# One order of work for the gate products, the decay steps and the fourth modulation sum of a hybrid RG-LRU / SGU / conv-FFN block

## What is computed

```python
mod = silu(c) @ w_ada + b_ada                      # six vectors of 1024
h = modulated_norm(x, norm_mix_g, shift1, scale1)
xr, gr, zu, zv, ga, gb = split(h @ w_in)
xr = causal_dwconv(xr, rnn_conv_w, rnn_conv_b)     # four taps
r = sigmoid(block_diag(xr, lru_w_a, lru_b_a))      # 8 heads, 128 x 128 each
i = sigmoid(block_diag(xr, lru_w_x, lru_b_x))
log_a = 8 * r * log_sigmoid(lam)
a = exp(log_a)
u = sqrt(-expm1(2 * log_a)) * (i * xr)
h_t = a_t * h_(t-1) + u_t                          # scan over the tokens
y_a = (h * gelu(gr)) @ w_branch_a
y_b = spatial_gating(gelu(zu), gelu(zv)) @ w_branch_b
x = x + gate1 * ((sigmoid(ga) * y_a + sigmoid(gb) * y_b) @ w_out)
# then the channel sub-layer: norm, up, conv(3), gelu * val, down, gate2, final norm
```

## Time and profile before

| | |
|---|---|
| time, median of 3 runs | 1642.93 us (1642.1 to 1643.86) |
| the profiled execution's own time | 1643.54 us |
| its span in the trace | 1641.8 us |
| busy, TensorE / its weight loads | 1572.3 us (96%) / 1296.6 us (79%) |
| busy, VectorE / ScalarE / GpSimd | 1104.0 us (67%) / 712.2 us (43%) / 347.8 us (21%) |
| mean granted TensorE clock | 0.976 |
| moved by DMA | 146.10 MB |

### The profile page before, as it was taken

How to read it: one execution, slowest core, us unless ns; L and a number is a source line. 1 busy time by engine, 2 the same in 40 slices (tenths; PEclk the granted TensorE clock), 3 DMA queues, 4 the chain that set the end, 5 groups by cost and what they waited for, 6 DMA issues and landing times.

```text
span 1641.8 us, 18632 instructions
## 1 busy us (share of the span) xinstructions
PE 1572.3 (96%) x6996; PEld 1296.6 (79%) x6996; DVE 1104.0 (67%) x1209; ACT 712.2 (43%) x974; POOL 347.8 (21%) x218
## 2 busy tenths in 40 slices
PE   5889999999999999998999899999999999999998
PEld 4667777778888888887887778888888888888886
DVE  6877888855565684465437986677667667567674
ACT  3446878744555461111123434334334334334436
POOL 0432433532222200000000411211221221121204
PEclk7789999999999999998999999999999999999999
DMA  9322222221233347666210012112111111211112
GB/s 355 120 77 64 75 74 74 71 87 54 91 103 103 103 135 228 205 189 209 93 52 26 20 52 77 40 54 63 51 46 58 58 46 52 65 39 52 52 45 103
DMA packets 154312, 146.10 MB, mean 89 GB/s; under 512 B 6672, under 2 KB 132976, under 8 KB 153584
## 3 DMA queue, kind: packets, MB, share of 16 engines
q1 hardware_dynamic: 154224, 144.91, 27.8%
HBM read 123.91 MB, written 20.97 MB: 88 GB/s over the span
## 4 chain that ended last, share of the span: by engine, by line
PE 75%; DVE 13%; issue 4%; ACT 3%; DMA 3%; POOL 1%; SPq 0%; POOLq 0%; ACTq 0%; DVEq 0%
PE ps L671 42%; PE ps L929 15%; PE ps L728 11%; DVE wop L1495 2%; DMA ada_ring<-in_w_ada 2%; DVE xc L1649 1%; PE ps L959 1%; PE ps L859 1%; PE ps L800 1%; DVE ti L1681 1%; PE ps L647 1%; DVE t3w L2015 1%; DVE m L1672 1%; PE ps L633 1%; PE ps L749 1%
## 5 line engine op out<-in xcount | busy, mean ns | idle before, releaser
L1495 DVE TENSOR_TENSOR wop<-raw,wop 128x512 fp32r<-128x512 f32 x423 | 320.1, 766 | 220.3 <-ACT wop L1007 217.7
L1007 ACT ACTIVATE wop<-raw 128x512 fp32r<-128x512 f32 x423 | 260.8, 626 | 476.4 <-PE ps L671 151.2
L671 PE MATMUL ps<-yq,wop 128*128 128x512 f32 x1716 | 419.9, 394 | 14.0 <-DVE wop L1495 7.2
L671 PEld LDWEIGHTS ps<-yq,wop 128*128 128x128 f32 x1716 | 326.3, 191 | 85.6 <-DVE hidw L1967 4.9
L929 PE MATMUL ps<-hid,wop 128*128 128x512 f32 x1056 | 241.1, 389 | 0.0
L929 PEld LDWEIGHTS ps<-hid,wop 128*128 128x128 f32 x1056 | 198.2, 188 | 41.2
L530 POOL TENSOR_TENSOR raw<-raw,raw 128x512 f32<-128x512 f32 x45 | 66.7, 1482 | 493.1 <-DVE wop L1495 444.2
L1989 DVE SCALAR_TENSOR_TENSOR xT<-ps,mod,xT 128x1024 f32<-128x1024 f32 x88 | 113.0, 1284 | 47.0 <-PE ps L929 46.0
L671 PE MATMUL ps<-t2q,wop 128*128 128x512 f32 x540 | 132.7, 395 | 6.3 <-DVE wop L1495 6.1
L671 PE MATMUL ps<-t4q,wop 128*128 128x512 f32 x540 | 131.0, 391 | 2.2 <-DVE ps L1508 2.0
L1967 DVE SCALAR_TENSOR_TENSOR hidw<-ps,pc,hidw 128x1023 f32<-128x1023 f32 x96 | 122.8, 1279 | 13.2 <-ACT hidw L1367 12.3
(11 more groups left out here) (214 smaller groups left out, 1826.5 us busy)
## 6 DMA issues: line engine op xcount, KB each, us to landing
raw<-in_w_in SPq DMA_DIRECT2D x96, 256.0 KB, 3.3
raw<-in_w_up SPq DMA_DIRECT2D x96, 256.0 KB, 2.8
ada_ring<-in_w_ada SPq DMA_DIRECT2D x32, 512.0 KB, 4.4
raw<-in_w_down SPq DMA_DIRECT2D x48, 256.0 KB, 2.9
gate_keep<-tg SPq DMA_DIRECT2D x16, 512.0 KB, 4.1
tg<-gate_keep SPq DMA_DIRECT2D x16, 512.0 KB, 6.7
xtok<-in_x SPq DMA_DIRECT2D x4, 1024.0 KB, 6.8
ada_h<-in_w_ada SPq DMA_DIRECT2D x8, 512.0 KB, 9.0
```

What stands on the lines that cost most here:

```text
L671: done = nc.tensor.matmul(bank, left[:, w, lk, :], right[:, x, rk, :], start=(first and w == 0 and x == 0), stop=(last and w == 1), skip_g ...
L1007: nc.scalar.activation(wop[n % 4][:, 0, :, :], raw[slot][:, :, :], ACT.Copy).then_inc(f_hi, 1)
L1495: V.tensor_tensor(wop[n % 4][:, 1, :, :], raw[slot_of[n][0]][:, :, :], wop[n % 4][:, 0, :, :].bitcast(F32), ALU.subtract).then_inc(f_lo, 1)
```

## The change

In the units that follow an R unit, the gate products go between P3 and P4 in place of P2 and P3, and with them `gate_pair` and `decay` from slot 3 to slot 4. `decay_root` goes from slot 1 to slot 2. On VectorE, `decay_square` goes from slot 6 to slot 1 of the next unit, behind the conv taps and their split, `gated_input` from slot 3 to slot 5, `scan_input` from slot 2 to slot 3, and the splits that stood together in slot 6 go back to their slots, between the joins. On ScalarE, `hi` of the next unit's product 1 goes inside `decay`. In the projections, the fourth weight load of a unit goes ahead of the gate's and of the modulation's loads on the queue, and the fourth vector (e=3) is spread over B1 and B2, its sum being moved from B2 to B3. No instruction is added or removed, and none changes its size. The diff, cut to its core:

```diff
@@ tables
+        SUMS_AT = {AT["A", 2]: 0, AT["A", 3]: 1, AT["B", 1]: 2, AT["B", 3]: 3}
@@ sync engine, loop over the units
                 if g is not None:
                     spill_gate(g, 1)
+                weights(pos, 3, 4)
                 if SEQ[now][0] in "AB":
                     gate_back(SEQ[now][1] + (4 if SEQ[now][0] == "B" else 0))
                 if now in ADA_AT:
-                    ada_pieces(ADA_AT[now], 2, 8)
-                weights(pos, 3, 4)
+                    ada_pieces(ADA_AT[now], 2, 6 if ADA_AT[now] == 3 else 8)
+                if SEQ[now] == ("B", 2):
+                    ada_pieces(3, 6, 8)
                 if pos in ADA_AT:
                     ada_pieces(ADA_AT[pos], 0, 2)
@@ tensor engine
-                m, b, e = prev_unit(now, "R"), V_BLOCK[now] if now in V_BLOCK else None, ADA_AT[now - 1] if now - 1 in ADA_AT else None
+                m, b, e = prev_unit(now, "R"), V_BLOCK[now] if now in V_BLOCK else None, SUMS_AT[now] if now in SUMS_AT else None
...
-                if m is not None and w == 3:
+                if m is not None and w == 4:
                     block_diag(m, past)
...
-                    if s == 1 and pos - 1 in ADA_AT:
-                        e = ADA_AT[pos - 1]
+                    if s == 1 and pos in SUMS_AT:
+                        e = SUMS_AT[pos]
@@ scalar engine
-            def decay(m):
+            def decay(m, weights, n):
...
                 nc.scalar.activation(th[:, :], la_a[:, :], ACT.Tanh, bias=la4n[:, m:m + 1],
                                      scale=la4n[:, m:m + 1]).then_inc(ach, 1)
+                weights(n)
                 act.wait_ge(ach, 2 * m + 1)
...
-                    hi(n0 + w + 3)
+                    if m is None or w < 5:
+                        hi(n0 + w + 3)
                     if m is not None and w == 1:
                         conv_high(m)
-                    if m_past is not None and w == 1:
+                    if m_past is not None and w == 2:
                         decay_root(m_past)
-                    if m is not None and w == 3:
+                    if m is not None and w == 4:
                         gate_pair(m, BANKS[(pos - 1) % 2])
-                        decay(m)
+                        decay(m, hi, n0 + 8)
+                    if m is not None and w == 6:
+                        hi(n0 + 9)
@@ vector engine, units
                 for w in range(7):
+                    if m is not None and w == 5:
+                        gated_input(m)
                     if w >= 4:
                         join(pos, w - 4)
...
+                    if m_past is not None and w == 1:
+                        decay_square(m_past)
                     if m_past is not None and w == 3:
+                        scan_input(m_past)
                         scan(m_past)
...
-                    if m is None or w < 4:
-                        lo(n0 + w + 3)
-                    elif w == 6:
-                        lo(n0 + 7)
-                        lo(n0 + 8)
-                        decay_square(m)
-                        lo(n0 + 9)
+                    lo(n0 + w + 3)
...
-                    if m_past is not None and w == 2:
-                        scan_input(m_past)
-                    if m is not None and w == 3:
-                        gated_input(m)
@@ vector engine, branch projections
-                    if w == 2 and pos - 1 in ADA_AT:
-                        mod_part(ADA_AT[pos - 1], BANKS[(pos - 1) % 2][0])
+                    if w == 2 and pos in SUMS_AT:
+                        mod_part(SUMS_AT[pos], BANKS[(pos - 1) % 2][0])
                     if pos in ADA_AT:
                         e = ADA_AT[pos]
-                        for k in range(4 * (w - 2), 4 * (w - 2) + 4) if e % 2 and w >= 2 else range(2 * w, 2 * w + 2) if e % 2 == 0 else ():
+                        late = 2 if e == 3 else 4
+                        for k in range(late * (w - 2), late * (w - 1)) if e % 2 and w >= 2 else range(2 * w, 2 * w + 2) if e % 2 == 0 else ():
                             ada_piece(e, k)
+                    if SEQ[pos] == ("B", 2) and w < 2:
+                        ada_piece(3, 4 + 2 * w)
+                        ada_piece(3, 5 + 2 * w)
```

## The result

| | before | after |
|---|---|---|
| time, median of 4 runs | 1643.09 us (1642.10 to 1643.86) | 1619.96 us (1619.49 to 1621.60) |
| the profiled execution's own time | 1643.54 us | 1621.60 us |
| its span in the trace | 1641.8 us | 1619.9 us |
| mean granted TensorE clock | 0.976 | 0.978 |

The account below looks back on a forecast made before the run. The prediction took a ring over VectorE, ScalarE and GpSimd as the R stage's bound. The ring's 10.8 us plus the fourth sum's 9.6 made 20.4 us off, from the median of 1642.9 to 1622.5 us; range 1616.5 to 1631.

Parts of the forecast that it names:

- The reading of the bound: R stage: the 24.07 us unit period is set by VectorE, ScalarE and GpSimd; TensorE's holes are only its shadow.
- the ring: R stage: almost gapless chain of steps over VectorE, ScalarE and GpSimd, from one unit's conv taps to the next's, 24.07 us.
- The ring's length: R stage after the change: 12.2 plus 10.24 us, taken as 22.5 a unit; eight units give 10.8 us less.
- the hole at P6: R unit on TensorE: P6 would wait for join 1, which ends about +19.6 where P6 could start at +19.04: 0.6 us.
- The fourth sum: Projections: moving the fourth column sum to B3 removes 5.8 us of wait and 3.8 of slow clock, 9.6 us less.
- The queue at nothing: A and B units: sending the fourth weight load ahead of gate loads and pieces was put at no gain or loss.
- the units behind at nothing, with 1 us either way: One or two units behind the R stage, finishing the last head: decay_square in their first slots costs nothing, give or take 1 us.
- TensorE is the bound again: Rival, R stage: VectorE and GpSimd meet less, ring under 21.76 us, 25.6 us less in all, 1617.3 us; chance 0.17.
- three meetings in a unit of the old order: R stage: VectorE and GpSimd already contend three times in every old unit, the argument against TensorE being the bound.
- The ring stays longer: Rival, R stage: decay_square still contested, 1.1 us more, ring 23.6 us, 12.7 us less in all, 1630.2 us; chance 0.15.
- Only one half works: Rival: either the ring gains nothing (1633.3 us) or the fourth sum waits or slows another transfer (about 1632); chance 0.08.
- Slower: Rival, R stage: GpSimd gets ahead at three more meetings, 1.14 us each, ring 25.9 us, 1646.3 us; chance 0.03.

Follow-up runs that it names:

- decay_only: Kernel before with only decay_square moved behind the conv's split and decay_root one slot later; gate products stay between P2 and P3: 1632.86 us, ratio 0.9938.
- products_back: Changed kernel with only the gate products put back between P2 and P3 on TensorE: 1624.09 us, ratio 0.9887 to before.
- products_only: Kernel before with only the gate products moved behind P3 on TensorE, ScalarE and VectorE as before: 1655.7 us, ratio 1.008.
- short_y: Changed kernel with GpSimd's product of scan and gelu gate cut to 16 of its 1024 columns, the others left without the gate: 1616.15 us, ratio 0.9838.
- queue_only: Kernel before with only the fourth weight load moved ahead of the gate's and modulation's loads on the queue: 1643.53 us, ratio 1.0005.
- sum_old_queue: Kernel before with the fourth vector spread over B1 and B2 and its sum in B3, fourth weight load left behind the pieces: 1633.39 us, ratio 0.9948.
- y_on_vector: Changed kernel with the product of scan and gelu gate moved from GpSimd to VectorE, between join 2 and the last split: 1615.62 us, ratio 0.984.
- the two halves: Two runs: kernel before with only the modulation and queue part, 1633.88 us; changed kernel with that part undone, 1630.18 us.

## Why the prediction was right

**The reading of the bound.** Right. `decay_only` leaves the gate products where they wait and gives 10.0 us, and `products_back` puts them back into the changed kernel and loses some 2. `products_only` removes the wait and costs 12.8, though partly by a new wait of its own. The waits of the earlier trace rows were the shadow of the ring.

**The ring's length.** Worked out as 22.4 and taken as 22.5; measured 22.49 (199.84 to 222.33). The first part, from the taps to the start of GpSimd's product behind the scan, was 12.2 in the sum and is 12.16 (212.00 - 199.84), the second 10.24 and is 10.33. The steps came as worked out: `decay_square` 1.23 forecast and 1.22 measured, the split behind join 0 about 2.3 and 2.31, the hole at P6 0.6 and 0.51. The eight units gave 10.97 us for a forecast of 10.8; the first interval is 21.76 and the other six 22.47 to 22.59.

The Trainium skill (SBUF — State Buffer, on who interferes with whom) has a VectorE instruction with two SBUF inputs and a GpSimd one that reads SBUF take a shared port pair as a lock that the first holds to its end. The trace after agrees at the five meetings from `L565` on (ends at 215.32, 216.47, 217.55, 218.69, 219.24). `short_y` falls to TensorE's 21.76 us, which fits too but doesn't prove the lock, as the weight sums behind the short product also start earlier.

**The fourth sum.** Forecast 9.6 us, 5.8 of wait and 3.8 of low clock; measured 9.70 between the two landmarks, 5.84 of idle time and 3.86 (61.95 - 58.09) of the same matmuls taking longer. The pieces are in place 13.7 us ahead where I had reckoned with over 15.

**The queue at nothing.** Right, by `queue_only` and `sum_old_queue`.

**What was off.** The term "the units behind at nothing, with 1 us either way" was mis-sized: ZV1 gave 1.49 us. I had asked only whether the added `decay_square` found room, and not what the moves free. The unit is 0.43 us ahead at P2 (6.24 in place of 6.67 us from its start), 0.98 at P3 (9.06 in place of 10.04) and 1.50 at P6, whose wait of 0.24 us for a join went too. Only the step from P2 to P3, some 0.5 us, is the root's later slot: a copy that P3 waits for no longer stands behind it. `decay_only`, which moves the root and `decay_square` alone, gives 0.60 in ZV1 and nothing at P2. The 0.43 at P2 is there in `products_back` too (6.24), so it comes with what that run has and `decay_only` hasn't, the new order of splits, joins, gates and `gated_input`. ScalarE starts its reading of the V tiles (L1186, now L1190) 2.76 us into the unit in place of 3.68, and P2's copy stands behind it:

```profile
325.54 1.94 ACT L1186 ACTIVATE vv<-ps 128x1024 f32<-128x1024 f32 x2
```

```profile
313.55 1.94 ACT L1190 ACTIVATE vv<-ps 128x1024 f32<-128x1024 f32 x2
```

The dependence of P3 on its copy was also missing from my expectation for `products_only`, which came out 7 us worse. With that term, 0.2 us on the ring, 0.1 on the sum, and 0.4 us that the part from O0 on gave back (its cause is open), 20.4 becomes 21.8 of the 21.9 us between the two profiled executions. The medians differ by 23.1; the profiled execution of after is the slowest of its four runs, and the 1.2 us between the two measures lie within the runs' own spread.

**The rivals.** "TensorE is the bound again" needed the meetings to cost 0.74 us less a unit. They didn't; one product moved from GpSimd to VectorE is enough for it, as `y_on_vector` shows. I had counted three meetings in a unit of the old order against this rival; the earlier trace rows show five (`gated_input`, L530, `decay_square`, L541 and the last split each end behind the other engine's), so that argument was stronger than I made it. "The ring stays longer" fell with `decay_square` at 1.22 us. "Only one half works" fell with the two halves. "Slower" happened, but in `products_only` and by another mechanism than the one named: not meetings on SBUF, but a copy behind the root.

## What to carry to other kernels

Several small waits of the busiest engine, one in each unit and all alike, may be the shadow of a ring over engines none of which is busy all the time (here VectorE for 84%, ScalarE for 80% and GpSimd for 42% of a unit). Follow the work from one unit's instruction to the same one in the next: if there is no gap, the period is the ring's, and only what shortens the ring helps. Moving the waiting instruction alone can lengthen it, as what now comes first has needs of its own. When VectorE and GpSimd are both in the ring, add up ends instead of durations, and ask whether an elementwise product needs GpSimd at all.

A sum that waits for transfers costs more than its wait where the clock falls behind it: here 5.8 us of idle time and 3.9 us more.

## What the runs showed of the hardware

- The arithmetic of a meeting of VectorE and GpSimd on SBUF holds to a few hundredths: the second ends 0.55 us (128x512 split, 0.69 alone) or 1.08 to 1.15 us (a GpSimd sum, 1.29 alone; a 128x1024 product, 1.22 alone) after the first ends. It was so in all five meetings listed above.
- The same product of 128x1024 takes 2.77 us on GpSimd (it ends 2.27 after the split under which it starts) and 1.55 on VectorE, where it still meets a weight sum, and on GpSimd it also stretched a split from 0.69 to 2.31 us. More work for the busier of the two made the kernel 5.9 us faster. The two engines still meet all through the unit (the split, `gated_input` and the product each end behind a weight sum), but nothing stands behind a holder of 2.77 us any more.
- After 5.8 us without work TensorE's granted clock was 0.50 in the stretches from 748.6 to 756, though TensorE was busy again in both the earlier trace rows. From the sum of e=2 to O0 the same matmuls took 3.86 us longer for it.
